# Rotary halves swapped by transfers within SBUF instead of by products with a signed permutation

## The chip, the cores and the metric

One core of one Trainium2 chip. The metric is the device time of one execution in microseconds (us). Lower is better.

## The reference, cut to what matters

One layer of a hybrid encoder, 2048 tokens, width 1024, all in float32. `proj = rmsnorm(x) @ w_in` is cut into the queries, keys, values and gate paths of three branches (A sliding window, B top-k sparse with an indexer, C cross-attention into a memory). The queries and keys of A, of B and of B's indexer, in heads of 64 channels, are rotated:

```python
def _rope(x, cos, sin):
    x1, x2 = jnp.split(x, 2, axis=-1)
    return jnp.concatenate([x1 * cos - x2 * sin, x2 * cos + x1 * sin], axis=-1)

a_q = _rope(a_q.reshape(b, s, SWA_HEADS, HEAD_DIM), cos, sin)     # 512 columns
a_k = _rope(a_k.reshape(b, s, SWA_KV_HEADS, HEAD_DIM), cos, sin)  # 128
b_q, b_k = _rope(...), _rope(...)                                 # 512, 64
b_qi, b_ki = _rope(...), _rope(...)                               # 256, 64
```

Then come the three attentions, the gates, `w_branch`, `w_out`, the residual and a last RMSNorm.

## The kernel before, in words

**Tiling.** The tokens go in four passes of T = 512 (`g` = 0 to 3, called here the first to the fourth pass). A *unit* is the product of 128 (at times 68) columns of a weight with the 512 tokens: channels on the partitions, tokens along the row, in one PSUM bank `PJ`. To keep float32's precision every operand is split into a high and a low part of type float32r, and a unit is `PRODUCTS` = 24 matmuls of 512 columns (`projected`, L871, the matmul at L893). `PJ` is a ring of three banks.

**Weights.** In the first pass SyncE loads a unit's raw weight (`load_raw`, L684, two transfers, L696), ScalarE makes the high part (`split_hi`, L981, L992) and GpSimd the low part (`split_lo`, L1232, L1238), two units ahead; SyncE stores the pair in DRAM (`store_pair`, L701). `load_raw(wt + 2)` waits until the low part of unit `wt` is made. In the later passes SyncE only loads the pairs (`load_pair`, L710), each half when TensorE has finished that half two units earlier. `loads_after(st)` (L712) does this for every step of kind "unit", in the order of the steps. SyncE issues all transfers of the kernel.

**The order of the work.** `order_of_work` (L78) writes one list of steps, and every engine walks it in that order and does its part of each. `turned` (L149) lays out a run of units that are turned afterwards: in each round it lists unit n, then, for unit n-1, "turn" (values), "rope", then work that is put beside it (`count`, one bit of the search for the top-k threshold, L1552; `select`, pieces of the selection, L1593; `finish`, which adds the output of the pass before to the residual rows, L1744), then "halve". There are three such runs in a pass, each followed by gate units (role `z`):

- the *key run*: kv, qi, qi, kiw, with `finish` of the pass before beside it from the second pass on (eight transposes into `TR`, then L1750, the rows' squares L1002, the row scale L1755, the store `out<-rows`). The indexer's scores follow;
- the *window run*: ak, av, q, q, q, q, with a `count` beside each. The attention of branch A follows;
- the *sparse run*: q, q, q, q, with `select` beside. The attention of branch B follows.

`ROPED` is all of these but av: 13 units a pass, 52 in all, numbered `st.k`.

**A rotated unit before the change.**

- VectorE `emptied` (L1507, L1510): `staged` (= `fT`, a ring of two) = PJ x sine, then `turn[k % 4]` = PJ x cosine, which frees the bank. `table` holds sine and cosine, repeated over the four blocks of 32 partitions.
- ScalarE `emptied` (L1093): `fH` = high part of `fT`. For kv and kiw ScalarE first copies the rows that are not rotated (L1089), and VectorE's L1507 waits for this.
- GpSimd `added` (L1248): `fL` = `fT` - `fH`, queued between the unit's two `split_lo`.
- TensorE at "rope", after unit n+1 (L924, L925): two matmuls of 512 columns with `swapR`, a permutation with signs that exchanges the 32-partition halves of each head, into one of the two `TR` banks. The same two banks take all transposes, "finish" ones too, in turn; `tr_free` counts when VectorE has read one.
- VectorE `rotated` (L1388, L1393): `turn` += `TR`.
- "halve": ScalarE copies the sum to its high parts (L1163; two copies, four for qi and ak), VectorE subtracts for the low parts (L1661).

Of the kernel before, what the change touches and what calls it, by code (L numbers as in the profile page):

```python
# [8 lines left out]
ALU = mybir.AluOpType  # L9
# [3 lines left out]
P = 128  # L13
# [4 lines left out]
T = 512  # L18
# [40 lines left out]
class Step:  # L59


    def __init__(self, kind, role=None, source=None, src=None, which=None, branch=None, g=None, i=None,
# [11 lines left out]
        self.tiles, self.kept, self.gates, self.stored = tiles, kept, None, None  # L74
# [3 lines left out]
def order_of_work():  # L78
# [8 lines left out]
    pj_freed, s_freed, x_freed, f_freed, swaps = [], [], [], [], []  # L87
# [61 lines left out]
    def turned(specs, beside=(), counting=None, selecting=None, tables=False, finishing=None):  # L149

        units = []
        for n_unit in range(len(specs) + 1):
# [6 lines left out]
            if n_unit:  # L159
                st = units[n_unit - 1]  # L160
                if st.role in ("av", "mv", "kv", "kiw"):
                    steps.append(Step("turn", unit=st, tr=take("tr")))
                    f_freed.append(("tr_full", n["tr"]))
# [15 lines left out]
                if st.role in ROPED:  # L179
                    steps.append(Step("halve", unit=st, k=st.k, tr=swaps[-1]))  # L180
# [227 lines left out]
    return steps, every, pj_bank, s_bank, s_freed, x_freed, f_freed, swaps  # L408


def hybrid_block(nc, x, mem, positions, g_in, w_in, attn_sinks, g_mem, w_mem_kv, w_branch, w_out,
                 g_final, out):
    steps, units, pj_bank, s_bank, s_freed, x_freed, f_freed, swaps = order_of_work()
# [8 lines left out]
    trig = nc.dram_tensor("trig", (NG, HD // 2, 2 * T), F32, kind="Internal").ap()  # L422
# [6 lines left out]
    with ctx:  # L429
# [66 lines left out]
        fH, fL = (sb(name, [P, T], F32R, p_at + 4096 + i * 2048) for i, name in enumerate(("fH", "fL")))  # L496
# [27 lines left out]
        identR, swapR = sb("identR", [P, P], F32R), sb("swapR", [P, P], F32R)  # L524
# [92 lines left out]
        def paired(ap, n):  # L617
# [15 lines left out]
            pv_done f_hi f_lo f_sin stack_hi stack_lo rel_used tables_out tables_in pool_x y_hi y_lo m_hi m_lo p_sub p_exp rden_ready rden_spread  # L633
# [7 lines left out]
        freed_by = {n: S[n] for n in ("act_pj", "dve_pj", "act_s", "dve_s", "p_exp", "pool_x", "tr_full")}  # L641
# [22 lines left out]

        def wait_free(eng, ring, index):

            if index >= 2:
                engine, value = ring[index - 2]
                eng.wait_ge(freed_by[engine], value)
# [13 lines left out]
        def _(sp):  # L683
# [44 lines left out]
            for st in steps:  # L728
# [10 lines left out]
                elif st.kind == "sines":  # L739

                    sp.wait_ge(S["sin_ready"], 2)
                    for i, of in enumerate((1, 0)):
                        sp.dma_start(trig.rearrange("g f n -> (g f) n")[:, i * T:(i + 1) * T], folded[of][:, :]).then_inc(S["tables_out"], 16)
                elif st.kind == "load_tables":

                    sp.wait_ge(S["tables_out"], 32)
                    if st.used:
                        sp.wait_ge(S["dve_pv"], st.used)
                    for quarter in range(4):
                        rows_at = slice(32 * quarter, 32 * quarter + 32)  # L750
                        sp.dma_start(table[rows_at, :, :].rearrange("p a n -> p (a n)"), trig[st.g]).then_inc(S["tables_in"], 16)
# [29 lines left out]
        def _(pe):  # L781
# [121 lines left out]
            for st in steps:  # L903
# [76 lines left out]
        def _(act):  # L980
# [96 lines left out]
            def emptied(st):  # L1077
# [7 lines left out]
                elif st.role in ROPED:  # L1085
                    lanes = rows_of(st)
# [36 lines left out]
            for st in steps:  # L1123
# [18 lines left out]
                elif st.kind == "sines":  # L1142

                    for i in range(2):
                        act.wait_ge(S["ang_ready"], i + 1)
                        nc.scalar.activation(folded[i][:, :], folded[i][:, :], ACT.Sin).then_inc(S["sin_ready"], 1)
                elif st.kind == "norm":
# [7 lines left out]
                elif st.kind == "halve":  # L1155
                    un = st.unit
                    act.wait_ge(S["tr_free"], st.tr + 1)
# [65 lines left out]
        def _(pool):  # L1223
# [17 lines left out]
            def added(st, first=0, last=PRODUCTS):  # L1241
# [41 lines left out]
            link(nc.gpsimd.memset(made[:, :], 0.0))  # L1283
            for q in range(4):
                to, other = made[:, 32 * q:32 * q + 32], 32 * q + (-32 if q % 2 else 32)
                link(nc.gpsimd.affine_select(out=to, in_=to, compare_op=ALU.not_equal, fill=1.0 if q % 2 else -1.0,
# [494 lines left out]
```

## Time and profile before

| | |
|---|---|
| median of 3 runs | 2755.79 us (2755.4 to 2760.68) |
| the profiled execution | 2759.88 us, its span 2758.1 us |
| granted TensorE clock, mean | 0.972 |
| TensorE busy | 2501.3 us, 91% |
| VectorE busy | 1749.0 us, 63% |
| ScalarE busy | 1395.1 us, 51% |
| GpSimd busy | 410.6 us, 15% |
| DMA | 399.32 MB, mean 145 GB/s |

The spans of the engines overlap. A matmul's listed duration (393 ns) overlaps its neighbour's; the chain that ended last lists what each took of the time, and there 24 of them take 5.44 us. A share of busy time is an average over stages with different limits.

### The profile page before, as it was taken

Reading aid. Unit: us, or ns where it says so; the run is one execution under the profiler, and the core shown is the slowest. Engines: PE = TensorE matmul, PEld = TensorE weight load, DVE = VectorE, ACT = ScalarE, POOL = GpSimd, SP = SyncE. Lnnn points to the kernel's source line nnn. Section 1 sums busy time; section 2 is a strip of 40 time slices with the busy share of each in tenths; the row PEclk is TensorE's granted clock in tenths of the full one; section 3 lists DMA queues with packets and bytes.
Section 4 is the critical chain, followed back from the end, with each engine's and each line's share of the span. In section 5 each row is a group of like instructions: output and inputs, shape, how many; then the busy total and the mean of one; then the engine's idle time right before and its main releaser. Section 6 shows DMA issues by size and latency. Waiting matters only on the chain.

```text
span 2758.1 us, 36858 instructions
## 1 busy us (share of the span) xinstructions
PE 2501.3 (91%) x12861; PEld 2076.0 (75%) x12861; DVE 1749.0 (63%) x3573; ACT 1395.1 (51%) x2817; POOL 410.6 (15%) x397
## 2 busy tenths in 40 slices
PE   5998999998899999998889999999988889888997
PEld 5776888776778888887767788888666677777776
DVE  6467666224667677226777878732578888776652
ACT  5455655343656444224656645523466674545541
POOL 5334253441010000100010010010000000000010
PEclk8999999999999999999999999999999999999999
DMA  5757585794443422565243331146423324211125
GB/s 170 227 170 223 166 274 169 230 295 149 160 159 130 160 93 69 181 223 181 89 158 108 132 120 47 54 163 226 171 96 122 115 87 164 71 54 47 61 89 187
DMA packets 172583, 399.32 MB, mean 145 GB/s; under 512 B 13808, under 2 KB 96752, under 8 KB 162416
## 3 DMA queue, kind: packets, MB, share of 16 engines
q1 hardware_dynamic: 172400, 396.96, 43.2%
q8 instruction: 105, 1.72, 0.3%
q14 instruction: 78, 0.64, 0.1%
HBM read 308.31 MB, written 88.60 MB: 144 GB/s over the span
## 4 chain that ended last, share of the span: by engine, by line
PE 53%; DVE 19%; ACT 16%; issue 10%; DMA 1%; POOL 1%; SPq 0%; DVEq 0%; ACTq 0%; POOLq 0%
PE bank L893 38%; PE TR L789 5%; PE PV L860 5%; ACT signs L1058 4%; ACT prob L1023 3%; ACT prob L1033 3%; ACT ptH L1047 2%; DVE nmx L1427 2%; DVE score L1675 2%; DVE ptL L1458 2%; PE bank L800 2%; PE bank L801 2%; DVE prob L1417 2%; DVE zs L1493 1%; ACT squared L1002 1%
## 5 line engine op out<-in xcount | busy, mean ns | idle before, releaser
L893 PE MATMUL bank<-hH,pairs 128*128 128x512 f32 (+1 forms) x3584 | 1157.6, 393 | 18.1 <-DVE zs L1525 7.6
L893 PEld LDWEIGHTS bank<-hH,pairs 128*128 128x128 f32 x3584 | 678.5, 191 | 156.7 <-issue 18.7
L893 PE MATMUL bank<-hL,pairs 128*128 128x512 f32 (+2 forms) x1792 | 703.4, 393 | 0.0
L1058 ACT ACTIVATE signs<-score,bits 128x384 int8<-128x384 f32 (+7 forms) x256 | 335.8, 1312 | 214.4 <-DVE bits L1558 201.3
L1458 DVE TENSOR_TENSOR ptL<-TR,ptH 128x512 fp32r<-128x512 f32 (+1 forms) x384 | 257.0, 671 | 283.0 <-ACT ptH L1047 280.1
L893 PEld LDWEIGHTS bank<-hL,pairs 128*128 128x128 f32 (+1 forms) x1792 | 343.2, 192 | 64.6
L1047 ACT ACTIVATE ptH<-TR 128x512 fp32r<-128x512 f32 (+1 forms) x384 | 219.5, 576 | 319.5 <-PE TR L789 318.6
L1539 DVE TENSOR_SCALAR_CACHE_REDUCE above<-score,bits 128x256 uint8<-128x256 f32 (+8 forms) x264 | 326.5, 1237 | 9.4
L789 PE MATMUL TR<-identR,prob 128*128 128x128 f32 x1480 | 233.3, 279 | 84.9 <-ACT prob L1033 51.3
L789 PEld LDWEIGHTS TR<-identR,prob 128*128 128x128 f32 x1480 | 180.0, 142 | 158.2 <-ACT prob L1033 65.0
L893 PE MATMUL bank<-ysH,pairs 128*128 128x512 f32 x768 | 257.2, 397 | 10.6 <-issue 5.8
L1238 POOL TENSOR_TENSOR pairs<-raw,pairs 128x512 fp32r<-128x512 f32 x164 | 218.0, 1339 | 314.2 <-ACT pairs L992 313.9
L860 PE MATMUL PV<-ptH,vS 128*64 128x256 f32 (+1 forms) x864 | 203.9, 309 | 18.1 <-DVE lower L1484 14.7
L1023 ACT ACTIVATE prob<-prob,lows 128x512 f32<-128x512 f32 (+8 forms) x256 | 189.6, 744 | 38.8 <-DVE lows L1417 38.6
L893 PEld LDWEIGHTS bank<-ysH,pairs 128*128 128x128 f32 x768 | 146.3, 191 | 40.0 <-issue 6.6
L893 PE MATMUL bank<-mergedH,pairs 128*128 128x512 f32 x512 | 167.1, 398 | 9.1 <-DVE hL L1635 4.8
L992 ACT ACTIVATE pairs<-raw 128x512 fp32r<-128x512 f32 x164 | 101.0, 622 | 125.8 <-DMA raw<-in_w_in 58.5
L893 PE MATMUL bank<-ysL,pairs 128*128 128x512 f32 x384 | 152.2, 396 | 0.0
L860 PE MATMUL PV<-ptL,vS 128*64 128x256 f32 x548 | 149.7, 282 | 0.0
L1255 POOL TENSOR_TENSOR merged<-merged,sg 128x512 f32<-128x512 f32 x56 | 76.5, 1370 | 454.1 <-DVE sg L1519 454.1
L860 PEld LDWEIGHTS PV<-ptH,vS 128*64 128x64 f32 (+1 forms) x864 | 123.2, 152 | 23.2 <-DVE lower L1484 17.4
L1248 POOL TENSOR_TENSOR fL<-fT,fH 128x512 fp32r<-128x512 f32 (+1 forms) x52 | 66.9, 1287 | 492.2 <-ACT fH L1093 492.0
(215 smaller groups left out, 3648.9 us busy)
## 6 DMA issues: line engine op xcount, KB each, us to landing
pairs<-w_split SPq DMA_DIRECT2D x444, 512.0 KB, 3.5
w_split<-pairs SPq DMA_DIRECT2D x74, 1024.0 KB, 5.0
raw<-in_w_in SPq DMA_DIRECT2D x106, 256.0 KB, 5.6
xs<-in_x SPq DMA_DIRECT2D x4, 2048.0 KB, 9.3
rows<-in_x SPq DMA_DIRECT2D x16, 512.0 KB, 5.0
table<-trig SPq DMA_DIRECT2D x48, 128.0 KB, 3.0
raw<-in_w_branch SPq DMA_DIRECT2D x24, 256.0 KB, 5.8
out<-rows SPq DMA_DIRECT2D x3, 2048.0 KB, 7.5
```

Source lines behind the costliest of these rows:

```text
L789: last = nc.tensor.transpose(bank, src, identR[first:first + k, first:first + k].bitcast(F32))
L860: last = nc.tensor.matmul(bank[0:v.shape[1], col], v, pr[:, p], start=(j == 0 and b == 0 and i == 0), stop=(last_block and i == len(pairs_ ...
L893: done = nc.tensor.matmul(PJ[st.u + half * up][0:min(st.width, P), 0:st.n_tok], lhs, rhs[:, row, 0:st.n_tok], start=(n % 12 == 0 and (up o ...
L992: nc.scalar.activation(hi_of(un)[:, half], blocks_of(raw[wt % 2][:, :, :], un)[:, half], ACT.Copy).then_inc(S["hi_ready"], 1)
L1023: nc.scalar.activation(part, part, ACT.Exp, bias=low, scale=-1.0, accum_out=sums[:, i, col:col + 1]).then_inc(S["p_exp"], 1)
L1033: last = nc.scalar.activation(held(it)[:, first + o:first + o + 256], SC[s][:, o:o + 256], ACT.Exp, bias=nmx[:, it.m % 2, i:i + 1], scale= ...
L1047: nc.scalar.activation(ptH[place][:, cols], TR[tr % 2][:, cols], ACT.Copy).then_inc(S["pt_hi"], 1)
L1058: nc.scalar.activation(signs[:, 0:keys], score[:, tt, 0:keys], ACT.Sign, bias=thr.bitcast(F32)[:, tt:tt + 1], scale=-1.0, accum_out=cnt[:, ...
L1238: nc.gpsimd.tensor_tensor(lo_of(un)[:, half], blocks_of(raw[wt % 2][:, :, :], un)[:, half], hi_of(un)[:, half].bitcast(F32), ALU.subtract) ...
L1255: nc.gpsimd.tensor_tensor(sum_m, sum_m, gate_of(st.gates[half]), ALU.add).then_inc(S["pool_x"], 1)
L1458: TT(ptL[place][:, cols], TR[tr % 2][:, cols], ptH[place][:, cols].bitcast(F32), ALU.subtract).then_inc(S["tr_free"], 1)
L1539: link(TS(above[:, 0:keys], score[:, tt, 0:keys], of.bitcast(F32)[:, tt:tt + 1], 0.0, compare, ALU.add, accum_out=cnt[:, tt:tt + 1]))
```

## The change

The matmuls at "rope", the copy to `fH`, the subtraction to `fL`, and the matrix `swapR` with the GpSimd instructions that build it are gone. In their place SyncE, right behind `loads_after` of the unit, waits for the sine product of that unit and issues four transfers of 32 partitions x 2 KB (two for kv and kiw), from `fT` to the exchanged block of a tile `swapped`, a ring of two in the place of `fH` and `fL`. VectorE adds `swapped` in place of `TR`. The signs go into the table: the blocks take sine and minus sine in turn, for which ScalarE makes one more tile and SyncE writes four parts of `trig` instead of two. The two buffers of `fT` are freed by the transfers, and "rope" takes no `TR` bank.

```diff
@@ order_of_work, turned
                 if st.role in ROPED:
-                    swaps.append(take("tr"))
-                    steps.append(Step("rope", unit=st, k=st.k, tr=swaps[-1], first=(st is units[0])))
-                    if st.role in ("kv", "kiw"):
-                        f_freed.pop()
-                    f_freed.append(("tr_full", swaps[-1] + 1))
+                    steps.append(Step("rope", unit=st, k=st.k, first=(st is units[0])))
+                    if st.role not in ("kv", "kiw"):
+                        f_freed.append([])
+                    n_swaps[st.k % 2] += 2 if st.role in ("kv", "kiw") else 4
+                    st.swapped = 16 * n_swaps[st.k % 2]
+                    f_freed[-1].append((f"swapped{st.k % 2}", st.swapped))
@@ hybrid_block
-        fH, fL = (sb(name, [P, T], F32R, p_at + 4096 + i * 2048) for i, name in enumerate(("fH", "fL")))
+        swapped = sb("swapped", [P, 2, T], offset=p_at + 4096)
...
+        def swap_halves(queue, un):
+
+            queue.wait_ge(S["f_sin"], un.k + 1)
+            if un.k >= 2:
+                queue.wait_ge(S["f_sum"], un.k - 1)
+            for q in range(rows_of(un).stop // 32):
+                other = q + 1 - 2 * (q % 2)
+                queue.dma_start(swapped[32 * q:32 * q + 32, un.k % 2, :],
+                                staged(un)[32 * other:32 * other + 32, :]).then_inc(S[f"swapped{un.k % 2}"], 16)
@@ block.sync
-                    sp.wait_ge(S["sin_ready"], 2)
-                    for i, of in enumerate((1, 0)):
+                    sp.wait_ge(S["sin_ready"], 3)
+                    for i, of in enumerate((folded[1], folded[0], folded[1], turns)):
...
                 elif st.kind == "unit":
                     loads_after(st)
+                    if st.role in ROPED:
+                        swap_halves(sp, st)
@@ block.tensor
-                elif st.kind == "rope":
-                    lanes = rows_of(st.unit)
-                    pe.wait_ge(S["tr_free"], st.tr - 1)
-                    pe.wait_ge(S["f_lo"], st.k + 1)
-                    bank = TR[st.tr % 2][lanes, :]
-                    nc.tensor.matmul(bank, swapR[lanes, lanes], fH[lanes, :], start=True, stop=False)
-                    nc.tensor.matmul(bank, swapR[lanes, lanes], fL[lanes, :], start=False, stop=True).then_inc(S["tr_full"], 1)
@@ block.scalar, emptied
-                    act.wait_ge(S["f_sin"], st.k + 1)
-                    if st.k:
-                        act.wait_ge(S["tr_full"], swaps[st.k - 1] + 1)
-                    nc.scalar.activation(fH[lanes, :], staged(st)[lanes, :], ACT.Copy).then_inc(S["f_hi"], 1)
@@ block.scalar, sines
+                    act.wait_ge(S["sin_ready"], 2)
+                    nc.scalar.activation(turns[:, :], folded[0][:, :], ACT.Copy, scale=-1.0).then_inc(S["sin_ready"], 1)
@@ block.gpsimd, added
-                if st.role in ROPED and last == PRODUCTS:
-                    lanes, f = rows_of(st), staged(st)
-                    pool.wait_ge(S["f_hi"], st.k + 1)
-                    nc.gpsimd.tensor_tensor(fL[lanes, :], f[lanes, :], fH[lanes, :].bitcast(F32), ALU.subtract).then_inc(S["f_lo"], 1)
@@ block.vector, rotated
-                dve.wait_ge(S["tr_full"], st.tr + 1)
+                dve.wait_ge(S[f"swapped{st.k % 2}"], st.unit.swapped)
                 dve.wait_ge(S["dve_pj"], st.unit.used)
-                TT(turn[lanes, st.k % 4, :], TR[st.tr % 2][lanes, :], turn[lanes, st.k % 4, :], ALU.add).then_inc(S["tr_free"], 1)
+                TT(turn[lanes, st.k % 4, :], swapped[lanes, st.k % 2, :], turn[lanes, st.k % 4, :], ALU.add).then_inc(S["f_sum"], 1)
```

## Rows read from the trace of the kernel before

**Rows 1.** The page: the chain that ended last, share of the span by engine

```profile
PE 53%; DVE 19%; ACT 16%; issue 10%; DMA 1%; POOL 1%; SPq 0%; DVEq 0%; ACTq 0%; POOLq 0%
```

**Rows 2.** Removed instructions by line: count, duration ns min/median/max, first and last start

```profile
L1093 ACT ACTIVATE fH<-fT x52: 615/632/635, 80.0 to 2336.6; 128x512 fp32r<-128x512 f32 x44, 64x512 fp32r<-64x512 f32 x8
...
L1248 POOL TENSOR_TENSOR fL<-fT,fH x52: 1260/1283/1678, 80.7 to 2337.3; 128x512 fp32r<-128x512 f32 x44, 64x512 fp32r<-64x512 f32 x8
```

**Rows 3.** Chain that ended last, sparse run, second pass: start, length (us), what

```profile
954.23 5.44 PE bank L893 x24
960.12 5.44 PE bank L893 x24
```

**Rows 4.** VectorE's timeline, sparse runs of passes three and four

```profile
1599.26 0.69 DVE L1507 TENSOR_TENSOR fT<-bank,table 128x512 f32<-128x512 f32 x1
1605.31 0.69 DVE L1507 TENSOR_TENSOR fT<-bank,table 128x512 f32<-128x512 f32 x1
...
2330.35 4.05 DVE L1604 TENSOR_TENSOR_SCAN flags<-flags 128x416 f16<-128x416 f16 x3
```

**Rows 5.** VectorE's, TensorE's and ScalarE's timelines, key run, second pass [idle before <-releaser]

```profile
653.30 0.69 DVE L1507 TENSOR_TENSOR fT<-bank,table 128x512 f32<-128x512 f32 x1 [3.42 <-PE bank L893]
...
655.33 0.63 PE L789 MATMUL TR<-identR,ob 128*128 128x128 f32 x4 [1.18 <-DVE turn L1393]
...
662.22 0.68 DVE L1507 TENSOR_TENSOR fT<-bank,table 64x512 f32<-64x512 f32 x1 [1.62 <-ACT fT L1089]
...
664.13 2.56 ACT L1163 ACTIVATE qst<-turn 64x512 fp32r<-64x512 f32 x4 [0.57 <-DVE turn L1393]
...
666.72 2.79 DVE L1661 TENSOR_TENSOR qst<-turn,qst 64x512 fp32r<-64x512 f32 x4 [1.05 <-ACT qst L1163]
...
672.67 1.29 DVE L1750 TENSOR_TENSOR rows<-TR,rows 128x512 f32<-128x512 f32 x2 [0.29 <-PE TR L789]
```

**Rows 6.** VectorE's timeline, window run, second pass

```profile
782.77 0.69 DVE L1507 TENSOR_TENSOR fT<-bank,table 128x512 f32<-128x512 f32 x1 [1.77 <-PE bank L893]
...
788.50 0.69 DVE L1393 TENSOR_TENSOR turn<-TR,turn 128x512 f32<-128x512 f32 x1 [4.44 <-PE TR L925]
789.11 0.15 DVE L1546 TENSOR_TENSOR bits<-small 128x4 int32<-128x4 f32 x1
...
805.25 0.95 DVE L1546 TENSOR_TENSOR bits<-small 128x4 int32<-128x4 f32 x1
```

**Rows 7.** SyncE's queue: issue ns min/median/max of the 128 KB table loads, and their landing

```profile
L751 SPq DMA_DIRECT2D table<-trig x48: 317/421/1551, 62.5 to 2303.1; - x48
...
DMA to landing us min/median/max: 2.1/3.0/6.9
```

**Rows 8.** SyncE's, VectorE's and ScalarE's timelines, first pass

```profile
68.86 1.34 SPq L701 DMA_DIRECT2D w_split<-pairs  x1
...
79.30 0.68 DVE L1507 TENSOR_TENSOR fT<-bank,table 64x512 f32<-64x512 f32 x1 [8.52 <-ACT fT L1089]
...
90.34 0.69 DVE L1507 TENSOR_TENSOR fT<-bank,table 128x512 f32<-128x512 f32 x1 [0.90 <-PE bank L893]
...
98.67 0.68 DVE L1507 TENSOR_TENSOR fT<-bank,table 64x512 f32<-64x512 f32 x1
...
220.79 3.79 DVE L1661 TENSOR_TENSOR wkB<-turn,wkA 64x512 fp32r<-64x512 f32 x4
...
376.20 0.34 SPq L701 DMA_DIRECT2D w_split<-pairs  x1
...
378.64 0.68 DVE L1507 TENSOR_TENSOR fT<-bank,table 128x512 f32<-128x512 f32 x1
...
383.45 1.50 SPq L696 DMA_DIRECT2D raw<-in_w_in  x2
...
389.53 0.63 ACT L992 ACTIVATE pairs<-raw 128x512 fp32r<-128x512 f32 x1 [2.70 <-DMA raw<-in_w_in]
```

**Rows 9.** By stretch, sparse run, first pass: us, busy by engine, clock, DMA share, GB/s

```profile
378.00:414.00 36.00, 36.00 (x167) 29.94 (x166) 24.17 (x38) 18.54 (x35) 23.07 (x18) 1.00 0.90 289
```

More of the change, by code:

```diff
@@ L73, in __init__ @@
         self.tr, self.p, self.pv, self.before, self.slots, self.behind = tr, p, pv, before, slots, behind
-        self.tiles, self.kept, self.gates, self.stored = tiles, kept, None, None
+        self.tiles, self.kept, self.gates, self.stored, self.swapped = tiles, kept, None, None, None
         self.scale, self.norm, self.woven, self.ring, self.read = scale, norm, woven, ring, read
@@ L86, in order_of_work @@
     count = dict(act_pj=0, dve_pj=0, act_s=0, dve_s=0, pool_x=0)
-    pj_freed, s_freed, x_freed, f_freed, swaps = [], [], [], [], []
+    pj_freed, s_freed, x_freed, f_freed, n_swaps = [], [], [], [], [0, 0]
     last_out, last_gates, places_of = None, [], {}
@@ L179, in turned @@
                 if st.role in ROPED:
-                    steps.append(Step("halve", unit=st, k=st.k, tr=swaps[-1]))
+                    steps.append(Step("halve", unit=st, k=st.k))
         if finishing is not None:
@@ L407, in order_of_work @@
     finish_last(NG - 1)
-    return steps, every, pj_bank, s_bank, s_freed, x_freed, f_freed, swaps
+    return steps, every, pj_bank, s_bank, s_freed, x_freed, f_freed
 def hybrid_block(nc, x, mem, positions, g_in, w_in, attn_sinks, g_mem, w_mem_kv, w_branch, w_out,
                  g_final, out):
-    steps, units, pj_bank, s_bank, s_freed, x_freed, f_freed, swaps = order_of_work()
+    steps, units, pj_bank, s_bank, s_freed, x_freed, f_freed = order_of_work()
     x_v = x[0].rearrange("(g t p) d -> g p t d", t=NT, p=P)
@@ L421, in hybrid_block @@
     mem_scratch = nc.dram_tensor("mem_scratch", (P, 4096), F32, kind="Internal").ap()
-    trig = nc.dram_tensor("trig", (NG, HD // 2, 2 * T), F32, kind="Internal").ap()
+    trig = nc.dram_tensor("trig", (NG, HD // 2, 4 * T), F32, kind="Internal").ap()
     once = sum(st.src == "w_mem_kv" for st in units)
@@ L523, in hybrid_block @@
         wmask = sb("wmask", [P, 2, 256], F32R)
-        identR, swapR = sb("identR", [P, P], F32R), sb("swapR", [P, P], F32R)
+        identR = sb("identR", [P, P], F32R)
         wi = sb("wi", [P, NT, 4])
@@ L640, in hybrid_block @@
         block = ctx.enter_context(nc.Block())
-        freed_by = {n: S[n] for n in ("act_pj", "dve_pj", "act_s", "dve_s", "p_exp", "pool_x", "tr_full")}
+        freed_by = {n: S[n] for n in ("act_pj", "dve_pj", "act_s", "dve_s", "p_exp", "pool_x", "tr_full", "swapped0", "swapped1")}
         def blocks_of(tile, un):
@@ L663, in gate_of @@
             return kept[:, st.m, :] if st.kept else sg[:, st.x % 2, :]
+        def swap_halves(queue, un):
[6 more added lines that the diff above has]
+                                staged(un)[32 * other:32 * other + 32, :]).then_inc(S[f"swapped{un.k % 2}"], 16)
         def wait_free(eng, ring, index):
             if index >= 2:
-                engine, value = ring[index - 2]
-                eng.wait_ge(freed_by[engine], value)
+                for engine, value in ring[index - 2] if type(ring[index - 2]) is list else [ring[index - 2]]:
+                    eng.wait_ge(freed_by[engine], value)
         def wait_bank(of_kind, index):
@@ L750, in _ @@
                         rows_at = slice(32 * quarter, 32 * quarter + 32)
-                        sp.dma_start(table[rows_at, :, :].rearrange("p a n -> p (a n)"), trig[st.g]).then_inc(S["tables_in"], 16)
+                        sp.dma_start(table[rows_at, :, :].rearrange("p a n -> p (a n)"),
+                                     trig[st.g, :, quarter % 2 * 2 * T:(quarter % 2 + 1) * 2 * T]).then_inc(S["tables_in"], 16)
                 elif st.kind == "unit":
                     loads_after(st)
+                    if st.role in ROPED:
+                        swap_halves(sp, st)
                 elif st.kind in ("index", "attention"):
@@ L1282, in _ @@
             pool.wait_ge(S["consts"], 1)
[L1283 to L1286, printed above, removed]
-                                             base=-other, pattern=[[-1, 32]], channel_multiplier=1))
-            link(nc.gpsimd.tensor_copy(swapR[:, :], made[:, :]))
             link(nc.gpsimd.memset(wmask[:, :, :].bitcast(F32), 0.0))
```

11 lines of the change are left out of this document (5 added, 6 removed).

## Prediction

> **What bounds the kernel now.** The chain that ended last is 53% TensorE, and VectorE and ScalarE hold 35% of it [rows 1]. So two matmuls saved are worth their time in some stretches and nothing in others, and each of the twelve runs with rotated units (three in each of four passes) has to be looked at by itself. The chain within a sparse run comes first [rows 3]: 24 matmuls take 5.44 us, the next unit begins 5.89 us after the last, and the 0.45 us between is the removed pair. There TensorE is the bound. Then VectorE's timeline where it is late: its sine products (L1507), one per unit, come 6.05 us apart in the third pass's sparse run [rows 4], 8.92 us apart in the key run of the second pass [rows 5]; these runs go by a chain through VectorE and ScalarE. Last SyncE's queue: in the first pass it is ahead of TensorE, and the DMA engines there are 0.90 busy [rows 9].
>
> **What is removed.** Per unit 0.45 us of TensorE, 0.63 us of ScalarE and 1.28 us of GpSimd [rows 2, 3]. All 52 pairs on the path would give 52 x 0.45 = 23 us. I go run by run.
>
> *Key run, passes two to four.* TensorE puts the product of the pair and two `finish` transposes into the two TR banks; the second transpose waits 1.18 us until VectorE has read the pair's product [rows 5], and the next unit stands behind it. Without the pair the banks are free and the unit starts some 2.5 us sooner. What is late next is VectorE's own loop: sine and cosine products and the sum 3 x 0.6 (they follow each other at 0.6), ScalarE's four copies 2.56, VectorE's four subtractions 2.79 [rows 5], 0.2 between them: 7.35 us. First interval 8.92: the sine product of 653.30 comes 0.7 sooner, the next one 7.35 later, at about 659.95 in place of 662.22. The gate unit's product comes another 7.35 later, and there the values' `turn` and the last residual additions (672.67, two, ended 673.96) end at some 669.9. That is 4.1 us off the end of the run; the squares, the row scale, the output's store and the indexer follow and move with it. Three times: -12.3.
>
> *Window run, passes two to four.* VectorE has a bit of the search in each unit, and TensorE waits. Its small `TENSOR_TENSOR` L1546 takes 0.15 alone and 0.95 in three of the rounds, where the removed GpSimd subtraction runs [rows 6]: 3 x 0.8 = 2.4. The sum of ak now follows 5.73 us behind its sine product (782.77 to 788.50), since the pair is queued behind the next unit. The new path is not in the trace: the product 0.69, three issues of 0.42 ahead of the last transfer, and its landing, bounded by the table loads of 32 partitions, 2.1 to 6.9, median 3.0 [rows 7]. I take the median, the nearest in kind and size: 5.0, so -0.7. With the ends it is 4.1 or 8.9, so -1.6 to +3. Together -3.1 each, -9.3.
>
> *Sparse run, passes two to four.* Pass two: 4 x 0.45 = -1.8. Pass three: VectorE's 6.05 sets the pace, only some 0.7 is left. Pass four: VectorE is the bound; a scan of the select runs in the place that L1546 had [rows 4], and I give it the same 0.8, in two rounds: -1.6. Together -4.1.
>
> The three sum to **-26**. In a running queue of rotated units the sum is due 5.44 + 1.2 = 6.6 us behind the start of its sine product, and the transfers need 5.0, so they lie beside other work; at the longest landing of 6.9 they would be 2.3 late.
>
> *First pass, SyncE's queue.* Here the change costs. Today SyncE issues as soon as the low part is made, before the unit is even multiplied: the store of qi's pair at 68.86, though kv's sine product starts at 79.30; in the sparse run a store and two loads at 376.20, before the first sine product at 378.64 [rows 8]. The new wait stands behind each rotated unit's loads, and behind it are queued the next unit's store and raw loads, the key run's and the sparse run's. A raw load lands 6.1 us after its issue (383.45 to 389.53 [rows 8]), and ScalarE waits for it in order: behind that wait stand its copies (L1163) and kiw's L1089, which the next sine product needs. So a loop closes: sine product 0.69, four issues 1.7, the store's 0.4, landing 6.1, two copies 1.2: 10.1 us, against 8.33 today in the key run (90.34 to 98.67 [rows 8]). With 2 us for the first delay and two such rounds: +6 for the key run. In the sparse run the first load is held back 4.5 us with its next partners, less 0.45 a unit: +4. The window run's rounds hold a bit of the search too and hide most: +2, less what the subtraction gave VectorE. Together **+12**. Bounds: all hidden, and the pairs saved, -3; 13 units each losing the excess of 2 us, +26. The transfers add 0.26 MB to a unit's 1.5, on engines 0.90 busy [rows 9]; that excludes the gain, mostly.
>
> *At nothing:* the third sine tile (0.63 of ScalarE) and two more table writes delay a table that is used at 79.30; its first load was issued at 62.5 [rows 7, 8], so 10 us cover them. The missing `swapR` instructions run ahead of everything. SyncE's issues in later passes (1.7 per unit) lie in its waits, and the pair loads behind them have their unit's 5.44 to spare.
>
> The sum read from two SBUF tiles instead of PSUM costs the same beside an idle GpSimd: L1661 reads two tiles, four in 2.79. In the first pass four took 3.79 [rows 5, 8], one being held up 1.0 while GpSimd made a low part. The Trainium skill ("SBUF — State Buffer", Who interferes with whom) says that a VectorE instruction with two SBUF inputs is blocked by a GpSimd one that reads SBUF, for its whole length, and this sum did not have two before; the trace agrees in that row. By it 13 sums of the first pass can each wait; by the rows I take 0 to 3 in the +12.
>
> **The sum:** -26 + 12 = -14 against the profiled execution's 2759.88: 2746. The median of the runs is 4.1 lower, so **2742**.
>
> **Rivals.**
>
> 1. *SyncE's wait costs nothing in the first pass.* For: two units of slack between load and use. Against: ScalarE already waits for these loads [rows 8]. -26 - 3: 2727.
> 2. *The VectorE loops don't shorten.* The sum waits for its transfers where it waited for TensorE, and of the key runs' 12.3 only the pairs (3 x 4 x 0.45 = 5.4) come off. Window runs 0, sparse -4.1, first pass +12: +2, no change: 2758.
> 3. *Slower: the first pass's loads.* The loop above runs in all 13 units of the pass, window run too, as swaps, stores and raw loads share full DMA engines: 2.9 us each, +38. Net +12: 2768. It decides from 26/13 = 2.0 us a unit on. For it: DMA share 0.90 [rows 9]. Against: the window run's rounds are longer than the loop.
> 4. *The shared port.* All 13 first-pass sums wait a whole GpSimd subtraction, 1.28 [rows 2]: +17 less the 3 taken, net 0: 2756. The page named above has the rule; against it, one of four instructions was held in the row, not all.
>
> **How the numbers follow.** Forecast 0.47, rival 1 0.20, rival 2 0.13, rival 4 0.05, rival 3 0.15. About 0.2% (5.5 us) is what a measurement of this kernel can tell from no change. Faster by more: nearly all of the forecast and rival 1, 0.65; within: rivals 2 and 4 and the forecast's edge, 0.20; slower: 0.15. The range takes rival 1 and a little below, and above it rivals 2 and 4 and the nearer half of rival 3: 2724 to 2764. The forecast's own is 2732 to 2752.
>
> **What would show it.** Right: in the chain units of the second sparse run 5.44 apart; residual additions of the second to fourth key run 4 us nearer to the run's start; L1546 at 0.15; the transfers landed before the sum is due, so VectorE not waiting for them save at ak; in the first pass longer waits of ScalarE for `raw`, and the indexer's start some 4 to 6 us later. Wrong, if VectorE waits for `swapped` in key and sparse runs, if the first pass ends at the same time or over 25 us later, or if the later passes are each not 6 to 10 us shorter.

## The result, and the profile after

| | kernel before | kernel after |
|---|---|---|
| median of the runs of this comparison, us | 2759.58 (2753.91 to 2762.51, 7 runs) | 2768.05 (2762.8 to 2772.03, 7 runs) |
| ratio of the times | | 1.0037, 95% interval [1.0024, 1.005] |
| profiled execution, us | 2759.88 | 2762.86 |
| its span, us, and granted clock | 2758.1, 0.972 | 2761.1, 0.968 |

The change makes the kernel 0.37% slower, more than the 0.2% that count as no change. The forecast was 2742 us with a range of 2724 to 2764: wrong in sign, and outside the range. The number that came is that of the third rival, 2768 us; its reason is not what the runs show (see the account of the prediction).

The page of the kernel after: busy time by engine, then the chain that ended last by engine and by line, the copies that take a raw block apart, and the transfers of raw blocks (count, size, median us to landing).

```profile
PE 2480.6 (90%) x12757; PEld 2060.5 (75%) x12757; DVE 1725.9 (63%) x3573; ACT 1364.1 (49%) x2766; POOL 343.0 (12%) x339
PE 49%; DVE 18%; ACT 17%; issue 9%; DMA 4%; SPq 1%; POOL 1%; DVEq 0%; ACTq 0%
PE bank L907 35%; ACT signs L1065 5%; PE TR L803 5%; PE PV L874 5%; ACT prob L1040 3%; ACT prob L1030 3%; DMA raw<-in_w_in 2%; DVE nmx L1421 2%; ACT ptH L1054 2%; DVE score L1669 2%; DVE ptL L1452 2%; PE bank L814 2%; PE bank L815 2%; DVE prob L1411 1%; DVE zs L1487 1%
...
L999 ACT ACTIVATE pairs<-raw 128x512 fp32r<-128x512 f32 x164 | 99.7, 621 | 177.2 <-DMA raw<-in_w_in 102.6
...
raw<-in_w_in SPq DMA_DIRECT2D x106, 256.0 KB, 5.6
```

TensorE's share of the chain is 49% where it was 53%, and that of DMA 4% where it was 1% [rows 1]. ScalarE stood idle for raw blocks 102.6 us; in the kernel before it was 58.5. A raw load took 5.6 us in both. So the loads did not get slower; they were asked for later.

**Where in the run the time went.** The start of each sine product (L1507 before, L1501 after) can be set beside its partner in the other trace. The difference, after less before, in us:

| | kv | kiw | ak | last q of the window run | first and last q of the sparse run |
|---|---|---|---|---|---|
| first pass | +0.3 | +4.0 | +9.8 | +11.8 | +16.0, +20.2 |
| second | +24.5 | +22.3 | +20.0 | +18.9 | +19.2, +18.3 |
| third | +17.3 | +15.3 | +13.0 | +11.9 | +11.3, +9.8 |
| fourth | +10.5 | +8.3 | +6.3 | +5.0 | +5.1, +3.4 |

The first pass loses 24.2 us, the later three give back 7.2, 6.8 and some 7.5, and 3 are left at the end, as the two profiled executions differ. The granted clock of the first pass fell too: 0.97 before (0 to 640 us), 0.95 after (0 to 664 us), with 41 and 68 us at the lower of the two levels, 1.2 GHz. (The medians differ by 8.5. Executions of one kernel lie some 4 us to either side of their median, so I take places and mechanisms from the traces and sizes from the medians where they disagree.)

**The first pass.** SyncE's timeline in the sparse run, as in [rows 8] of before:

```profile
388.12 0.34 SPq L712 DMA_DIRECT2D w_split<-pairs  x1
388.50 1.49 SPq L707 DMA_DIRECT2D raw<-in_w_in  x2
395.38 2.42 SPq L673 DMA_DIRECT2D swapped<-fT  x4
397.84 0.58 SPq L712 DMA_DIRECT2D w_split<-pairs  x1
398.47 1.57 SPq L707 DMA_DIRECT2D raw<-in_w_in  x2
```

and ScalarE's, with the idle time before each step:

```profile
395.23 1.15 ACT L999 ACTIVATE pairs<-raw 128x512 fp32r<-128x512 f32 x2 [4.84 <-DMA raw<-in_w_in]
405.34 1.15 ACT L999 ACTIVATE pairs<-raw 128x512 fp32r<-128x512 f32 x2 [8.96 <-DMA raw<-in_w_in]
```

Four issues of 0.6 us stand between the sine product and the store, the store's own issue takes 0.58 where it took 0.34, and the raw block issued at 398.47 is the one that ScalarE begins at 405.34 after 8.96 us of idleness. In the key run the chain (start, us, what) shows the loop as the prediction had drawn it: sine product, four issues, store, raw load, ScalarE's copies, next sine product, 11.62 us from start to start:

```profile
91.07 0.70 DVE fT L1501
...
91.79 0.52 SPq L673
...
94.70 0.58 SPq L712
...
95.83 5.56 DMA raw<-in_w_in
...
102.07 0.60 ACT fT L1095
...
102.69 0.69 DVE fT L1501
```

In the sparse run of before, from 370 to 425, 73.9% of the chain is TensorE's matmuls (L893):

```profile
by line: PE bank L893 73.9%; ACT prob L1023 4.8%; DVE ptL L1458 3.8%; ACT ptH L1047 3.3%; issue 3.2%; PE TR L789 3.0%; DVE prob L1417 2.1%; DVE zs L1493 1.7%; PE TR L925 1.6%; PE TR L924 1.6%; PE bank L801 0.4%; PE bank L800 0.4%; ACTq L991
```

Here, from 380 to 445, 39.2% is the raw loads:

```profile
by line: DMA raw<-in_w_in 39.2%; POOL pairs L1242 12.5%; DMA raw<-in_w_branch 9.1%; issue 5.8%; ACT pairs L999 5.0%; SPq L673 3.9%; DVE small L1595 3.0%; ACT prob L1030 2.8%; SPq L707 2.7%; DVE flags L1598 2.6%; DVE qst L1655 2.2%; DVE fT L
...
388.97 6.23 DMA raw<-in_w_in
...
395.94 2.55 POOL pairs L1242 x2
...
398.97 6.35 DMA raw<-in_w_in
...
415.69 0.70 DVE fT L1501
...
420.25 5.89 DMA raw<-in_w_branch
```

Only the load at 420.25 stands there behind the issues that follow a sine product. The two before it stand behind GpSimd's low part, for which `load_raw` waits: load, copy, low part, issue, 10.0 us from load to load. Once the loads are late, this second loop carries the lateness on.

**The later passes.** TensorE in the second pass's sparse run, in the same view of the chain (compare [rows 3]): one unbroken piece, 110 matmuls at 0.227 each, 5.44 for 24; the 0.45 between units is gone.

```profile
969.82 24.95 PE bank L907 x110
```

VectorE in the key run of the second pass, and in the window run (compare [rows 5, 6]):

```profile
677.19 0.69 DVE L1501 TENSOR_TENSOR fT<-bank,table 128x512 f32<-128x512 f32 x1 [2.99 <-PE bank L907]
...
684.51 0.68 DVE L1501 TENSOR_TENSOR fT<-bank,table 64x512 f32<-64x512 f32 x1
...
802.72 0.69 DVE L1501 TENSOR_TENSOR fT<-bank,table 128x512 f32<-128x512 f32 x1 [1.77 <-PE bank L907]
...
808.96 0.69 DVE L1387 TENSOR_TENSOR turn<-swapped,turn 128x512 f32<-128x512 f32 x1 [4.96 <-DMA swapped<-fT]
...
825.72 0.15 DVE L1540 TENSOR_TENSOR bits<-small 128x4 int32<-128x4 f32 x1
```

The sine products are 7.32 apart where they were 8.92; ak's sum comes 6.24 behind its sine product where it came 5.73 behind (third pass 6.15 and 5.73, fourth 5.24 and 4.93); the small step (L1546 before, L1540 after) takes 0.15 where it took 0.95.

### The profile page after: what moved, and what is told of

Its sections match the earlier page's. It is cut to its first block, busy times and chain, and to the rows that moved or that the text cites. A ratio compares the mean times of both kernels' runs of the same rounds, so it can differ in the third digit from the quotient of the medians.

```text
span 2761.1 us, 36678 instructions
## 1 busy us (share of the span) xinstructions
PE 2480.6 (90%) x12757; PEld 2060.5 (75%) x12757; DVE 1725.9 (63%) x3573; ACT 1364.1 (49%) x2766; POOL 343.0 (12%) x339
## 4 chain that ended last, share of the span: by engine, by line
PE 49%; DVE 18%; ACT 17%; issue 9%; DMA 4%; SPq 1%; POOL 1%; DVEq 0%; ACTq 0%
PE bank L907 35%; ACT signs L1065 5%; PE TR L803 5%; PE PV L874 5%; ACT prob L1040 3%; ACT prob L1030 3%; DMA raw<-in_w_in 2%; DVE nmx L1421 2%; ACT ptH L1054 2%; DVE score L1669 2%; DVE ptL L1452 2%; PE bank L814 2%; PE bank L815 2%; DVE prob L1411 1%; DVE zs L1487 1%
## 5 line engine op out<-in xcount | busy, mean ns | idle before, releaser
L1030 ACT ACTIVATE prob<-prob,lows 128x512 f32<-128x512 f32 (+8 forms) x256 | 189.6, 744 | 39.2 <-DVE lows L1411 38.9
L999 ACT ACTIVATE pairs<-raw 128x512 fp32r<-128x512 f32 x164 | 99.7, 621 | 177.2 <-DMA raw<-in_w_in 102.6
L907 PEld LDWEIGHTS bank<-ysH,pairs 128*128 128x128 f32 x768 | 146.2, 191 | 43.3 <-issue 10.1
L1513 DVE SCALAR_TENSOR_TENSOR sg<-sg,bank 128x512 f32<-128x512 f32 x56 | 38.4, 686 | 153.6 <-PE bank L907 153.4
```

The costliest lines, as they stand in the source:

```text
L907: done = nc.tensor.matmul(PJ[st.u + half * up][0:min(st.width, P), 0:st.n_tok], lhs, rhs[:, row, 0:st.n_tok], start=(n % 12 == 0 and (up o ...
L999: nc.scalar.activation(hi_of(un)[:, half], blocks_of(raw[wt % 2][:, :, :], un)[:, half], ACT.Copy).then_inc(S["hi_ready"], 1)
L1030: nc.scalar.activation(part, part, ACT.Exp, bias=low, scale=-1.0, accum_out=sums[:, i, col:col + 1]).then_inc(S["p_exp"], 1)
```

## The experiments

After the two traces I held this theory (W, or C when the first runs had narrowed it): in the first pass SyncE's queue is part of the loop that feeds the next unit, and the wait with the issues behind it, put in front of the store and the raw loads, is what costs. The rivals: the transfers' own traffic on busy DMA engines, and their landing before VectorE's sum. All times are medians; each is compared with runs of the kernel before on the same chip. Runs 1 to 3 share one chip, 4 and 6 to 8 a second, 5, 9 and 10 a third; where kernels of two chips are set side by side, each one's difference from before on its own chip is what counts.

**1. The same swaps, issued one unit later in the first pass.**

```diff
 elif st.kind == "unit":
     loads_after(st)
-    if st.role in ROPED:
-        swap_halves(sp, st)
+    while pending:
+        swap_halves(sp, pending.pop())
+    if st.role in ROPED and st.g == 0:
+        pending.append(st)
+    elif st.role in ROPED:
+        swap_halves(sp, st)
```

> The changed kernel, but in the first pass alone SyncE issues a unit's transfers behind the next unit's store and raw loads instead of in front of them. Theory W (the first pass lost its 24 us because the wait for the sine product held back the store and the raw loads queued behind it): the first pass comes back to within 5 us of the kernel before, the later passes keep their gain of 21 us, and the whole is 16 to 24 us shorter than before (ratio 0.991 to 0.994). Rival D (the transfers' own traffic and issue time on a full queue): they are all still there, so the first pass stays 15 us or more behind and the whole lies at 0.998 to 1.004. Rival L (late landing of the transfers holds VectorE): worse than the changed kernel, since they are issued later.

Measured 2741.29 us (2727.49 to 2747.32), ratio 0.9937 [0.9917, 0.9958]. That is 15.2 us less than before, where 16 to 24 were expected. ScalarE's idle time for raw blocks fell to 58.1, what it was before the change; the second pass's kv is 8.9 us late instead of 24.5, where at most 5 were expected. The same transfers with the same bytes, put behind the loads, give back most of the loss. The 8.9 us that are left are not explained; eight of VectorE's 13 first-pass sums were longer than usual there, by 5.7 us together, which may be a part of them.

**2. The first pass as before, with its matmuls; transfers in the later three.**

```diff
+def by_transfer(g):
+    return g > 0
...
+                if st.role in ROPED and by_transfer(st.g):
+                    swap_halves(sp, st)
...
+                elif st.kind == "rope" and st.k in old:
...
+                    nc.tensor.matmul(bank, swapR[lanes, lanes], fH[lanes, :], start=True, stop=False)
+                    nc.tensor.matmul(bank, swapR[lanes, lanes], fL[lanes, :], start=False, stop=True).then_inc(S["tr_full"], 1)
```

> The first pass rotated as in the kernel before (copy, subtraction, two matmuls), the later three passes by transfers. All theories agree that the first pass is as before; it measures what the later passes gain by themselves: 21 us by the two traces, forecast 26, so 0.990 to 0.993. If it is above 0.997 the gain of the later passes in the traces was given back elsewhere.

Measured 2732.76 us (2729.88 to 2735.16), ratio 0.9915 [0.9901, 0.993]. That is within what was expected. Its trace runs 4.0 us ahead of before's at the first sine product, 3.6 at the last of the first pass, 26.0 at the last of the fourth and 24.7 at the end of the span: by it the later passes are worth 21 to 22.

**3. The wait alone, and the traffic alone.** Both are the kernel before with its matmuls. One makes SyncE wait for the sine product behind a rotated unit's loads of the first pass; the other issues as many transfers of 64 KB at that place, without the wait, from an input to memory that nothing reads.

```diff
 loads_after(st)
+if st.role in ROPED and st.g == 0:
+    sp.wait_ge(S["f_sin"], st.k + 1)
```

```diff
 loads_after(st)
+if st.role in ROPED and st.g == 0:
+    for q in range(rows_of(st).stop // 32):
+        sp.dma_start(extra[4 * st.k + q], w_in[0][32 * q:32 * q + 32, 0:T]).then_inc(S["extra_out"], 16)
```

> The kernel before, with one thing added: in the first pass SyncE waits for the sine product behind each rotated unit's store and loads. No transfer is issued and the matmuls stay. Theory W: most of the first pass's loss appears, +12 to +24 us (1.004 to 1.009). Rival D: nothing, within 3 us of the kernel before.

> The kernel before, with one thing added: in the first pass SyncE issues, behind each rotated unit's store and loads and without a wait, four transfers of 32 rows x 2 KB (two for kv and kiw) from an input to a scratch tensor in DRAM. It adds the number of transfers, their bytes and their issue time, and no order. Theory W: 0 to +5 us. Rival D: +12 us or more (1.004 and up).

The wait alone: 2758.42 us, ratio 1.0009 [0.9998, 1.0019]. The traffic alone: 2755.87 us, ratio 1.0 [0.9991, 1.0009]. Neither costs anything that can be measured (both intervals hold 1), so the theory in the form of the wait alone fell, and so did the traffic. It fell clearly: in the sparse run the DMA engines had been 0.90 busy [rows 9], and the added transfers made them 1.00 busy (same view, last two numbers DMA share and GB/s):

```profile
376.00:412.00 36.00, 36.00 (x166) 29.93 (x166) 24.15 (x39) 18.34 (x35) 23.75 (x18) 1.00 1.00 313
```

These transfers go from memory to memory outside SBUF. They stand for the number, the bytes and the issue time of the swaps; the swaps' own path was tested by runs 1 and 6.

**4. Wait and issues together.** Both edits at once, so that the transfers are issued behind the wait and in front of the next store and loads. The matmuls stay and nothing waits for the transfers to land.

```diff
 if st.role in ROPED and st.g == 0:
+    sp.wait_ge(S["f_sin"], st.k + 1)
     for q in range(rows_of(st).stop // 32):
         sp.dma_start(extra[4 * st.k + q], w_in[0][32 * q:32 * q + 32, 0:T]).then_inc(S["extra_out"], 16)
```

> The kernel before, matmuls and all, with SyncE in the first pass waiting for the sine product behind a rotated unit's loads and then issuing as many transfers of 64 KB as the unit has quarters; they carry an input's rows to memory outside SBUF that nothing reads. So the wait and the issues stand together in front of the store and the next raw loads, as in the changed kernel, but no engine waits for the transfers to land. Theory C (it is the sum of the two that moves the raw loads: 1.9 to 2.9 us of issue behind a wait that was free by itself): 13 units lose 1.2 to 1.9 us each, +15 to +24 us, 2771 to 2781 us. Rival L (the time is lost where VectorE's sum waits for the transfers to land, 1.9 to 5.0 us, and what follows the sum): nothing waits here, so the time is that of the wait alone, 2756 to 2760 us.

Measured 2781.11 us (2778.29 to 2785.12), ratio 1.0086 [1.0073, 1.0099]: 23.7 us more than before's 2757.46. That is the upper end of what theory C said, and as much as the first pass lost, without one transfer that the kernel uses. SyncE's timeline and the waits of ScalarE (us in total, times, longest) of this kernel:

```profile
391.06 2.41 SPq L758 DMA_DIRECT2D extra<-in_w_in  x4
393.52 0.57 SPq L702 DMA_DIRECT2D w_split<-pairs  x1
394.14 1.50 SPq L697 DMA_DIRECT2D raw<-in_w_in  x2
...
ACT pairs L997 <- DMA raw<-in_w_in: 102.9, 28, 8.1
```

The pattern, and the 102.9, are those of the changed kernel.

**5. Half the issues.** The same with two transfers for a unit of 128 rows and one for a unit of 64.

```diff
-    for q in range(rows_of(st).stop // 32):
+    for q in range(rows_of(st).stop // 64):
```

> e7_wait_issue with half the transfers behind each wait of the first pass: two for a unit of 128 rows, one for one of 64, 0.5 to 1.1 us of issue in place of 1.1 to 2.3. The wait alone gave 2758.4 us, with all the issues it was 2781.1. Theory C1 (the raw loads start later by every 0.6 us of issue, and each such 0.6 us is paid in full): halfway, 2768 to 2771 us. Theory C2 (the first issues go into slack of the loop, about 1 us a unit, and only what lies beyond it is paid): nearer the wait alone, 2759 to 2765 us.

Measured 2774.37 us (2769.98 to 2776.55), ratio 1.0062 [1.0049, 1.0074]. With the runs of 3 and 4 this gives the cost by what stands behind the wait:

| behind the wait, first pass | time less before | ScalarE idle for raw blocks (before: 58.5) |
|---|---|---|
| nothing | +1.9 | 81.9 |
| half the issues | +16.7 | 92.5 |
| all the issues | +23.7 | 102.9 |

Neither form of the expectation held. C2, a free first microsecond, is out: the first half costs more than the second, 14.8 against 7.0. C1, each issue paid in full, holds for the first half (24 issues of some 0.59 are 14.2 us) and not for the second. The three medians come from three chips and each is uncertain by some 3 us, so that the first half costs more is likely rather than certain. I read it so: the wait alone took 23 us of ScalarE's spare time and cost almost nothing, and the loads that come still later have no spare time left. That reading is argued from the idle times; no run tests it by itself. Nor does one separate what the lower clock costs: in the first pass TensorE spent 41 us at 1.2 GHz before, 44 with the wait alone, 38 with the traffic alone, 65 with both and 68 after the change. It goes with the loss, so it looks like part of how the loss is paid and not like another cause.

**6. The first pass's swaps issued from GpSimd's queue,** at the place of its old subtraction.

```diff
-                    if st.role in ROPED:
+                    if st.role in ROPED and st.g:
                         swap_halves(sp, st)
...
+                if st.role in ROPED and last == PRODUCTS and st.g == 0:
+                    swap_halves(nc.gpsimd, st)
```

> The changed kernel, but in the first pass the swaps are issued from GpSimd's queue, at the place of its old subtraction, so that SyncE's queue there holds neither wait nor issue for them. The transfers, their landing and the sum that waits for them stay. Theory C: the first pass loses no more than 4 us against before, and the later passes give back their 20: 2738 to 2745 us. Rival L: the landing is no shorter from this queue, so the first pass keeps its 24 us and the time stays at 2758 to 2770 us.

Measured 2739.8 us (2736.59 to 2744.66), ratio 0.9939 [0.9927, 0.9952]. The swaps, their landing and the sum that waits for them are all there; only SyncE's queue is free of them, and most of the loss is gone (second pass's kv +4.5, ScalarE's idle time for raw blocks 65.9). The 48 swaps took 2.9 us to land in the median, no less than the 2.5 of SyncE's, so the landing is ruled out as what costs. The Trainium skill ("DMA: Bandwidth & Descriptors", Issuing engines are not separate DMA queues) says that issuing from several engines saves only the time it takes the sequencer to initiate a transfer, "usually small relative to the DMA itself". Here one issue took 0.59 us where the swap had landed after 2.5, and four of them stood behind a wait. Moved off SyncE's queue, wait and issues together were worth some 26 us: 17.7 less than before against 8.5 more, or 1.0% by the two ratios.

**7. The first pass's loss without the later gain:** transfers in the first pass, matmuls in the later three (`by_transfer` of run 2 with `g == 0`).

> Transfers in the first pass only; in the later three the splits and products by ones of the kernel before. If what the first pass lost (24.5 us by the two traces) is lost for good, the time is 2756 + 24 = 2780 us (2776 to 2784). Rival: the later passes had time to spare at the places where VectorE got faster, and part of the 24 us is caught up again there whatever the rotated units do: 2764 to 2772 us, and then the gain of the later passes would be smaller than the 20 us read from the traces.

Measured 2782.34 us (2774.8 to 2787.7), ratio 1.0086 [1.0071, 1.0101]: 24.9 us more than before. Nothing of it is caught up later: its trace stands 24.9 late at the second pass's kv and 27.2 at the last sine product. It is also the time of run 4 on the same chip, so the swaps in use, with their matmuls gone, add nothing net to the wait and the issues.

**8. A subtraction on GpSimd put back,** in the later passes of run 1's kernel. It is two instructions of 256 columns, reads a constant, and its result is unused.

```diff
+                if st.role in ROPED and last == PRODUCTS and st.g:
+                    pool.wait_ge(S["f_sin"], st.k + 1)
...
+                        nc.gpsimd.tensor_tensor(junk[lanes, :], mask, mask, ALU.subtract).then_inc(S["f_back"], 1)
```

> The kernel of e1_defer with a subtraction on GpSimd put back in each rotated unit of passes 2 to 4, at the place of the old one and as wide (two halves of 256 columns, reading a constant, its result unused); nothing waits for it. If GpSimd's reading of SBUF beside VectorE's small steps was what cost 0.8 us each, the window runs lose 2.4 us each again, +5 to +8 us against e1_defer's 2741.3: 2746 to 2749 us. Rival: the 0.8 us came from elsewhere (the order of the old copy and split), and the time stays within 2 us of e1_defer's: 2739 to 2743 us.

Measured 2751.21 us (2745.32 to 2757.12), ratio 0.9976 [0.9968, 0.9985]: 9.9 us above run 1, or 9.0 by the differences from before (6.3 and 15.2 us less), where 5 to 8 were expected. The small step's line in VectorE's timeline, window run of the second pass:

```profile
808.32 0.57 DVE L1555 TENSOR_TENSOR bits<-small 128x4 int32<-128x4 f32 x1
```

It takes 0.57 nine times in the later passes, beside the second GpSimd piece of 256 columns (0.94 us there, 0.61 elsewhere); in the kernel before it took 0.91 to 0.95 at the same nine places, beside one piece of 512 columns and 1.26 to 1.29 us; in the changed kernel 0.15. All 18 times the step ended 16 to 20 ns after GpSimd's piece did, however long it had waited. That GpSimd was the cause of the 0.8 is shown. The step reads two tiles of SBUF, as does GpSimd's subtraction, and the rule of the Trainium skill ("SBUF — State Buffer", Who interferes with whom) agrees. The 9 us are more than 9 x 0.4; the profiled execution, one of the faster ones, shows only 3 more than run 1's from the second pass's kv to the last sine product. What the rest is stays open. The granted clock is a candidate: its mean over the executions was 0.9675 here and 0.972 in run 1.

**9. All swaps from GpSimd's queue, and run 2 with its swaps from there.**

```diff
-                    if st.role in ROPED:
-                        swap_halves(sp, st)
...
+                if st.role in ROPED and last == PRODUCTS:
+                    swap_halves(nc.gpsimd, st)
```

> The changed kernel with the swaps of all four passes issued from GpSimd's queue, none from SyncE's. In passes 2 to 4 SyncE's queue was not what anything waited for, so taking the swaps off it should give nothing there: as e8_pool_queue's 2739.8, 2736 to 2744 us. Rival: GpSimd's own issues use SBUF as its subtraction did, beside VectorE's small steps in the window runs, and the 2.4 us a pass come back: 2745 to 2749 us.

> e2_first_old (matmuls in the first pass, transfers in the later three), with the later transfers issued from GpSimd's queue. By the same reason as e10_pool_all the place of issue does not matter in the later passes: e2_first_old's 2732.8, 2730 to 2736 us. Rival: the sum in the window and sparse runs, which waited 0.5 us longer for the transfers than for the matmuls, comes sooner or later by the queue's own landing time: 0.5 us in 6 units a pass, up to 9 us either way.

Measured 2750.4 us, ratio 0.9974 [0.9962, 0.9985], and 2746.49 us, ratio 0.9961 [0.9946, 0.9975]: 10.6 and 13.7 us above run 6 and run 2. Both expectations missed. By the differences from before it is 10.4 over run 6, and 10.1 over run 10, which is run 2 on the same chip. The place of issue does matter in the later passes, and GpSimd's is the worse. One cause is in VectorE's timeline of the first of the two, at ak's sum:

```profile
782.75 0.69 DVE L1501 TENSOR_TENSOR fT<-bank,table 128x512 f32<-128x512 f32 x1 [1.77 <-PE bank L905]
783.36 0.68 DVE L1504 TENSOR_TENSOR turn<-bank,table 128x512 f32<-128x512 f32 x1
790.33 0.69 DVE L1387 TENSOR_TENSOR turn<-swapped,turn 128x512 f32<-128x512 f32 x1 [6.29 <-DMA swapped<-fT]
```

The sum comes 7.58, 7.33 and 7.07 us behind its sine product in the three passes, in run 6 6.22, 5.74 and 5.09: 4.9 us together. In the second kernel it is 8.16, 8.00 and 7.97 against run 10's 6.27, 5.20 and 4.81: 7.9 us. It is not the small step, which stays at 0.15. The other 6 and 2 us are not shown. Here too the granted clock is a candidate: its mean was 0.9684 and 0.9685 in the two kernels, 0.9724 in run 6 and 0.971 in run 10, and in the profiled executions TensorE spent 143 and 137 us of the later passes at 1.2 GHz against 92 and 116. Among the executions of the kernel before, on the two chips where its clock varied enough to tell, 0.001 of clock went with 1.1 us; an estimate from that gives 3 to 5 us for these differences. Whether the clock is a cause or follows from TensorE's waits is not shown.

**10. Run 2 once more.**

> e2_first_old once more, beside the others on one chip: if its gain is real the ratio is again 0.991 to 0.992 of before; were it the chip or the moment of that run, it would lie nearer 0.995.

Measured 2736.4 us (2728.96 to 2737.3), ratio 0.9917 [0.9902, 0.9932]. This version, matmuls in the first pass and transfers issued by SyncE in the others, is the best that I found: 0.8% faster than before, 1.2% faster than the change.

## Why the prediction was wrong, point by point

- **Key runs of the later passes, -4.1 each: right, 13.0 in all where 12.3 were forecast.** The offsets shrink by 4.5, 4.3 and 4.2 from kv to ak, and the interval forecast at 7.35 is 7.32.
- **Window runs, -3.1 each: right in its larger part, wrong in the smaller.** The 3 x 0.8 came, and run 8 shows the cause. ak's sum was put 0.7 sooner; it is 0.3 to 0.5 later, 6.24 in place of 5.0 in the second pass, since an issue took 0.59 and not the 0.42 of [rows 7], which leaves some 3.7 for the last landing, not 3.0. That leaves -1.9 each. The upper end given, 8.9, held it.
- **Sparse runs, -4.1 together: a little high, 2.8.** The pauses of 0.45 are gone; some of that is given back in the attention in front of them. The fourth pass's scans are at 3.32 where they took 4.05, the forecast 0.8.
- **Later passes in sum:** forecast -26, by the traces -21.5, by run 2 without the first pass -23.8 and -21.2. The second rival, that VectorE's loops don't shorten, is out.
- **First pass, +12: the step that failed,** half the size it should have had. Its mechanism was named: the store and the raw loads queued behind the wait, then the landing, then ScalarE's copies in order, then the next sine product. It was the size. By the offset of each run's last sum the key run lost 6.7 (forecast 6), the window run 6.6 (forecast 2), the sparse run 10.9 (forecast 4); run 7 puts the whole at 24.9. Two steps of the working fell. *"The window run's rounds hold a bit of the search too and hide most":* before, the sine products there stood 5.4, 10.3 and 9.5 apart (224.61 to 249.86), and the loop, forecast at 10.1, is longer than two of the three. *"The first load is held back 4.5 us", once, in the sparse run:* the lateness does not come once; the chain there goes on through loads behind the low parts, and one more behind a sine product's issues. And the loop itself is 11.6 us, not 10.1 (91.07 to 102.69 in the key run), since the four issues take 2.9 there and the store 0.58, not 1.7 and 0.4. The window and the sparse run each have one interval as long (242.38 to 253.84, 398.27 to 410.21).
- **The third rival's 2768 came by luck.** It had the loop in all 13 units, 2.9 us each, +38, and -26 for the rest. The first pass lost 24.9 (1.9 a unit, below the 2.0 from which it was to decide, and by few long intervals, not in every unit), and the later passes gave 21.5. So the change is worth +8.5 and not its +12, and the kernel before, 3.8 us slower by seven executions than by three, makes up the rest. Its reason, full DMA engines, fell with the added traffic (run 3). It was right that the window run does not hide the loop. The sentence against it, that the window run's rounds are longer, could have been refuted by the trace of before: I compared the loop with no interval there.
- **The baseline:** 2742 was counted from the 2755.79 of three executions; with seven the kernel before is at 2759.58. Of the 26 us of the miss 3.8 are this.
- **The reason behind it was only half right.** The prediction blamed the wait, and counted the issues as one term of the loop. By runs 3 to 5 the wait is free alone and the issues are free alone; what costs is issues behind a wait.
- **DMA share of 0.90** was taken to exclude a gain and to speak for full DMA engines. The added traffic costs nothing (run 3), with the engines 1.00 busy in the same stretch.
- **The first rival,** 2727 or 29 us less than before, is not reached even with the swaps out of SyncE's first-pass queue: run 6 gives 17.7 less. Where 3 us were to be saved in the first pass, its trace is 4.0 later at the second pass's kv than at the first sine product.
- **The shared port, fourth rival:** of the first pass's 13 sums one took 1.68 where 0.67 is usual, one 1.12, three 0.77 to 0.79: 1.8 us together, not 17. In run 6 seven of the 13 were held, three of them at 1.66 to 1.73, 4.1 us together, and the time was still 26 us better. The rule holds instruction by instruction; that every sum meets a subtraction does not.
- **At nothing:** kv's first sine product of the first pass was 0.3 late, so the third sine tile and the table writes were hidden.

## What to carry to other kernels

An in-order queue that runs ahead has slack until it is made to wait; here the wait took the slack at no cost, and the issues behind it were then paid, 14.8 us for the first 24 and 7.0 for the other 24. So cost a wait together with everything that is issued between it and the next load that somebody needs, and compare the loop with the actual interval in each run, not only in the one where it looks worst. When a transfer depends on compute, put its issue behind the loads of the next unit or on another queue, or leave it out of the stage where the loads are late: the same change was worth -0.8% in three passes and +0.9% in the first.

## What the runs showed of the hardware that I had not expected

A 64 KB transfer from SBUF to SBUF takes SyncE longer to issue than the 128 KB table loads did, 591 ns in the median against 421, and the store behind them took 0.58 where it took 0.34 without. Why the table loads are shorter is not shown. (Count, ns min/median/max, then landing:)

```profile
L673 SPq DMA_DIRECT2D swapped<-fT x192: 512/591/1427, 80.3 to 2341.8; - x192
...
DMA to landing us min/median/max: 1.9/2.5/5.0
```

In run 4 four transfers that go to memory outside SBUF took 2.41 too, so it is not the swap's kind of transfer that makes it. And 3.1 MB more (48 transfers) in the first pass, on engines that were 0.90 busy in its sparse run and 1.00 with them, did not move the time. A VectorE instruction of 0.15 us that reads two tiles of SBUF ended with the GpSimd subtraction beside it in 18 of 18 places, whether it began 0.9 or 0.57 us before that end.
